# Two alternating places for the first two gate/up chunks, and two experts per loop turn on TensorE and SyncE, in a hybrid decoder step

## The reference

```python
logits = (h @ router_w).astype(jnp.float32) + router_b.astype(jnp.float32)
top_vals, top_idx = lax.top_k(logits, TOP_K)            # 4 of 32 experts per token
gates = jax.nn.softmax(top_vals, axis=-1)
def expert_block(args):
    xb, e = args
    gu = xb @ w_gate_up[e] + b_gate_up[e]               # 1024 x 2048
    g = jnp.minimum(gu[:, :D_FF], SWIGLU_LIMIT)
    u = jnp.clip(gu[:, D_FF:], -SWIGLU_LIMIT, SWIGLU_LIMIT)
    act = (u + 1) * g * jax.nn.sigmoid(SWIGLU_ALPHA * g)
    return act @ w_down[e] + b_down[e]                  # 1024 x 1024
```

## Time and profile before

| | |
|---|---|
| median of the runs | 1736.56 us (1729.86 to 1739.68) |
| the profiled execution's own time | 1735.41 us |
| its span, first to last instruction | 1733.7 us |
| TensorE busy | 1474.0 us (85%), 11950 matmul instructions |
| share of 16 DMA engines, SyncE's queue | 81.9% |
| moved | 598.10 MB, mean 345 GB/s |
| granted TensorE clock, mean | 0.903 of full speed |

### The profile page before, as it was taken

The page is one execution under the profiler, slowest core; times in us unless marked ns, Lnnn a source line. Parts: engine busy times, 40 slices in busy tenths (PEclk is TensorE's granted clock), DMA queues, the critical chain, the costliest instruction groups (busy, mean ns, idle before and its releaser), DMA issues.

```text
span 1733.7 us, 32093 instructions
## 1 busy us (share of the span) xinstructions
PE 1474.0 (85%) x11950; PEld 595.0 (34%) x11951; DVE 782.4 (45%) x1160; ACT 356.0 (21%) x822; POOL 96.7 (6%) x173
## 2 busy tenths in 40 slices
PE   3868887779788978899998998999899999899970
PEld 2433333346433354332332332333233332232320
DVE  2789879997786335221332232132132131131326
ACT  3212212222222111111211211212112122121220
POOL 0000010000000000000100000000000000000000
PEclk8989995679898857999999999999899999999995
DMA  9557888988998785598999999999999999999986
GB/s 327 182 187 258 283 295 272 331 279 292 311 301 270 242 352 207 227 392 339 429 420 403 427 417 396 412 418 411 392 421 412 401 428 411 397 428 399 428 351 253
DMA packets 127292, 598.10 MB, mean 345 GB/s; under 512 B 20503, under 2 KB 20517, under 8 KB 102026
## 3 DMA queue, kind: packets, MB, share of 16 engines
q1 hardware_dynamic: 109088, 560.20, 81.9%
q10 hardware_dynamic: 8634, 20.00, 3.4%
q0 software_dynamic: 9504, 17.06, 2.6%
HBM read 589.36 MB, written 25.87 MB: 355 GB/s over the span
## 4 chain that ended last, share of the span: by engine, by line
PE 40%; DMA 19%; DVE 2%; issue 1%; ACT 0%; DVEq 0%; SPq 0%; ACTq 0%
PE bank L1511 25%; DMA wts<-in_w_gate_up 16%; PE bank L1548 8%; PE bank L1530 4%; DMA wts<-in_w_down 3%; PE bank L1501 1%; PE bank L1618 1%; DVE v_ring L2139 1%; PE bank L1559 1%; PE bank L1599 0%; DVE q_b L2139 0%; DMA h_tok<-h_rows,v_tok 0%; ACT k_T L1155 0%; DVEq L2127 0%; ACT k_T L1138 0%
## 5 line engine op out<-in xcount | busy, mean ns | idle before, releaser
L1511 PE MATMUL bank<-wts,h_T 128*32 128x512 f32 x4032 | 443.9, 597 | 9.7 <-DMA wts<-in_w_gate_up 5.2
L2061 DVE TENSOR_SCALAR q_T<-bank 128x512 f32<-128x512 f32 x32 | 22.1, 692 | 636.9 <-PE bank L1511 636.9
L1511 PEld LDWEIGHTS bank<-wts,h_T 128*32 128x32 f32 x4032 | 129.5, 111 | 308.3 <-issue 296.4
L1548 PE MATMUL bank<-wts,k_T 128*32 128x512 f32 x2048 | 228.3, 597 | 8.0 <-issue 4.9
L1530 PE MATMUL bank<-wts,h_T 128*32 128x512 f32 x992 | 132.6, 675 | 52.2 <-DMA wts<-in_w_gate_up 50.4
L1658 DVE TENSOR_TENSOR wts<-wts,q_b 128x1024 f32<-128x1024 f32 x128 | 158.1, 1235 | 23.1 <-DMA wts<-in_cache_k 17.4
L1661 DVE TENSOR_REDUCE sc<-wts 128x16 f32<-128x1024 f32 x128 | 156.2, 1220 | 4.4
L1145 ACT ACTIVATE h_T<-bank 128x512 f32<-128x512 f32 x66 | 35.9, 595 | 573.5 <-PE bank L1501 573.5
L1548 PEld LDWEIGHTS bank<-wts,k_T 128*32 128x32 f32 x2048 | 64.9, 110 | 149.0 <-issue 139.5
L1223 PE MATMUL bank<-wts,h_T 128*8 128x128 f32 (+1 forms) x480 | 92.7, 465 | 12.3 <-ACT h_T L854 6.4
L1155 ACT ACTIVATE k_T<-bank 32x256 f32<-32x256 f32 x256 | 95.7, 374 | 13.6 <-PE bank L1548 10.2
(11 more groups left out here) (330 smaller groups left out, 1375.8 us busy)
## 6 DMA issues: line engine op xcount, KB each, us to landing
wts<-in_w_gate_up SPq DMA_DIRECT2D x126, 2048.0 KB, 15.8
wts<-in_w_down SPq DMA_DIRECT2D x64, 2048.0 KB, 18.3
wts<-in_cache_k SPq DMA_DIRECT2D x256, 256.0 KB, 3.7
v_ring<-in_cache_v SPq DMA_DIRECT2D x160, 256.0 KB, 3.8
wts<-in_cache_v SPq DMA_DIRECT2D x96, 256.0 KB, 3.9
wts<-in_w_in SPq DMA_DIRECT2D x5, 2048.0 KB, 24.1
wts<-y_rows SPq DMA_DIRECT2D x4, 2048.0 KB, 15.1
wts<-in_w_out ACTq DMA_DIRECT2D x8, 512.0 KB, 6.2
```

Of the source, the lines that this page charges most:

```text
L1511: m = nc.tensor.matmul(PS[part][p0:p0 + 32, :], lhs[:, 32 * b:32 * b + 32], rhs[:, part * F + half * 512:part * F + half * 512 + 512], sta ...
L1548: m = nc.tensor.matmul(PS[4][p0:p0 + 32, :], act_T[0][:, k, a0:a0 + 32], chunk[c][:, k, n * 512:(n + 1) * 512], start=(c == 0 and k == 0), ...
```

## The change

Chunks 0 and 1 of gate/up get a second place each: even places of the order use the old ones, odd places `v_ring` and `mix`, with semaphores of their own (`w_odd`). SyncE may therefore load chunks 0 and 1 of place i as soon as place i-2 has used them. Chunks 2 and 3 and both down chunks have one place, as before; place 1 now has its chunks 0 and 1 loaded early instead of 2 and 3. As the place in memory now depends on the parity of i, the bodies of SyncE's and TensorE's loops are written out for two places of the order per turn. The read of the size moves ahead of the two waits of a block. The last two down chunks wait for place 30 instead of place 31, and the residual rows for place 31's use of chunk 0. Five pairs of semaphores are merged (`rows_in`), to make room.

```diff
+        w_odd = [sem(f"w_odd{n}") for n in range(2)]
+        gu_full = [w_full[0:4], w_odd + w_full[2:4]]
...
-        gu_chunk = [w_slot[CHUNK_SLOT[c]].rearrange("p (k n) -> p k n", k=2) for c in range(4)]
-        first_gu = gu_chunk[0:2] + [v_flat.rearrange("p (k n) -> p k n", k=2),
-                                    mix[:, 0:SLOT].rearrange("p (k n) -> p k n", k=2)]
+        gu_even = [w_slot[CHUNK_SLOT[c]].rearrange("p (k n) -> p k n", k=2) for c in range(4)]
+        gu_odd = [half.rearrange("p (k n) -> p k n", k=2) for half in (v_flat, mix[:, 0:SLOT])] + gu_even[2:4]
+        gu_chunks = [gu_even, gu_odd]
...
-            def load_gate_up(i, e):
+            def load_gate_up(i, e, odd=0, ahead=0):
                 for c in range(4):
-                    sp.wait_ge(w_used[c], i)
-                    load_chunk(c, e)
+                    sp.wait_ge(w_used[c], i - ahead if c < 2 else i)
+                    load_chunk(c, e, odd)
...
             load_chunk(0, 0)
             load_chunk(3, 0)
+            load_chunk(0, 1, 1)
...
-            for c in range(2, 4):
-                sp.wait_ge(w_full[c], 16)
-                load_chunk(c, 1, first_gu)
+            load_chunk(1, 1, 1)
...
+            sp.wait_ge(meta_out, 2)
+            e = expert_at(2)
             for c in range(2):
                 sp.wait_ge(w_used[c], 1)
-                load_chunk(c, 1)
-            sp.wait_ge(meta_out, 2)
-            e = expert_at(2)
+                load_chunk(c, e)
             for c in range(2, 4):
                 sp.wait_ge(w_used[c], 1)
-                sp.wait_ge(w_full[c], 32)
-                load_chunk(c, e)
-            for c in range(2):
+                load_chunk(c, 1, 1)
+            for c in range(2, 4):
                 sp.wait_ge(w_used[c], 2)
                 load_chunk(c, e)
             load_down(1, 1)
-            with sp.Fori(3, E) as i:
-                load_gate_up(i, expert_at(i))
-                load_down(i - 1, expert_at(i - 1))
+            with sp.Fori(3, E - 1, 2) as i:
+                for odd in (1, 0):
+                    load_gate_up(i + 1 - odd, expert_at(i + 1 - odd), odd, 1)
+                    load_down(i - odd, expert_at(i - odd))
             e = expert_at(E - 1)
+            load_gate_up(E - 1, e, 1, 1)
+            load_down(E - 2, expert_at(E - 2))
             for q in range(2):
-                sp.wait_ge(w_used[q], E)
+                sp.wait_ge(w_used[q], E - 1)
...
+            sp.wait_ge(w_used[0], E)
             sp.wait_ge(x2_out, 16 * (TILES + 1))
...
-                    pe.wait_ge(w_full[c], i * 16 + 16)
+                    pe.wait_ge(gu_full[odd][c], loads if c < 2 else i * 16 + 16)
                     for k in range(2):
-                        m = products(hg_T[:, 2 * c + k, :], chunk[c][:, k, :], c == 0 and k == 0, False)
+                        m = products(hg_T[:, 2 * c + k, :], gu_chunks[odd][c][:, k, :], c == 0 and k == 0, False)
...
-            def expert_block(i, before=None, front=gate_up_front, back=gate_up_back):
+            def expert_block(i, before, odd, loads):
...
+                size = size_of(i)
                 after(pe, gclip_done, i * 2)
                 pe.wait_ge(xt_copied, i * 2 + 2)
-                size = by_size(front, back, i)
+                by_size(front, back, i, size)
...
-            expert_block(1, 0, first_gate_up_front, first_gate_up_back)
-            with pe.Fori(2, E) as i:
-                expert_block(i, i - 1)
+            expert_block(1, 0, 1, 16)
+            with pe.Fori(2, E, 2) as i:
+                expert_block(i, i - 1, 0, i * 8 + 16)
+                expert_block(i + 1, i, 1, i * 8 + 16)
```

More of the change, by code:

```diff
@@ L341, in hybrid_step @@
         v_full = [sem(f"v_full{n}") for n in range(VRING)]
-        xw_loaded = [sem(f"xw_loaded{n}") for n in range(TILES + 1)]
+        rows_in = [sem(f"rows_in{n}") for n in range(TILES + 1)]
         win_in = [sem(f"win_in{n}") for n in range(5)]
         w_full = [sem(f"w_full{n}") for n in range(6)]
+        w_odd = [sem(f"w_odd{n}") for n in range(2)]
+        gu_full = [w_full[0:4], w_odd + w_full[2:4]]
         w_used = [sem(f"w_used{n}") for n in range(6)]
-        y_loaded = [sem(f"y_loaded{n}") for n in range(TILES + 1)]
         last_full = [sem(f"last_full{n}") for n in range(2)]
@@ L566, in _, with load_chunk @@
                                                     for part in a_no})
-            def load_chunk(c, e, chunk=gu_chunk):
+            def load_chunk(c, e, odd=0):
                 if c < 4:
@@ L573, in load_chunk @@
                         "a (p k) n -> (a p) k n", p=P)[:, 2 * c:2 * c + 2, :]
-                    sp.dma_start(chunk[c], src).then_inc(w_full[c], 16)
+                    sp.dma_start(gu_chunks[odd][c], src).then_inc(gu_full[odd][c], 16)
                 else:
@@ L1502, in transpose_x, with gate_up_front @@
                     m.then_inc(xt_full, 1)
-            def gate_up_front(i, chunk=gu_chunk):
+            def gate_up_front(i, odd, loads):
                 def products(lhs, rhs, start, stop):
@@ L1522, in gate_up_front, with gate_up_back @@
                 products(sel[0:96, :], b_split[0:96, :], False, True).then_inc(gu_done, 1)
-            def gate_up_back(i, b, chunk=gu_chunk):
+            def gate_up_back(i, b, odd, loads):
                 def products(lhs, rhs, start, stop):
@@ L1534, in gate_up_back @@
                 for c in range(4):
-                    pe.wait_ge(w_full[c], i * 16 + 16)
+                    pe.wait_ge(gu_full[odd][c], loads if c < 2 else i * 16 + 16)
                     for k in range(2):
-                        products(hg_T[:, 2 * c + k, :], chunk[c][:, k, :], c == 0 and k == 0, False)
+                        products(hg_T[:, 2 * c + k, :], gu_chunks[odd][c][:, k, :], c == 0 and k == 0, False)
                 pe.wait_ge(sel_done, i + 1)
@@ L1579, in late_down_back, with size_of, by_size @@
                 down_back(i, b, loads=-1)
-            def by_size(front, back, i, size=None):
-                if size is None:
-                    size = pe.value_load(n_tok[0:1, bass.ds(i, 1)], min_val=0, max_val=CAP)
+            def size_of(i):
+                return pe.value_load(n_tok[0:1, bass.ds(i, 1)], min_val=0, max_val=CAP)
+            def by_size(front, back, i, size):
                 with pe.If(size > 64):
@@ L1589, in by_size @@
                 front(i)
-                return size
             def enter_late():
@@ L1601, in enter_late, with front, back @@
                 m.then_inc(late_summed, 1)
-            def expert_block(i, before=None, front=gate_up_front, back=gate_up_back):
+            def expert_block(i, before, odd, loads):
+                def front(i):
+                    gate_up_front(i, odd, loads)
+                def back(i, b):
+                    gate_up_back(i, b, odd, loads)
+                size = size_of(i)
                 after(pe, gclip_done, i * 2)
                 pe.wait_ge(xt_copied, i * 2 + 2)
-                size = by_size(front, back, i)
+                by_size(front, back, i, size)
                 transpose_x(i + 1)
@@ L1612, in expert_block @@
                 if before is not None:
-                    down_block(before, isinstance(i, int))
+                    down_block(before, isinstance(i, int) and i < 2)
                 for part in range(2):
@@ L1623, in down_block @@
             def down_block(i, first, front=down_front, back=down_back, size=None):
+                if size is None:
+                    size = size_of(i)
                 pe.wait_ge(at_copied, i * 2 + 2)
@@ L1645, in _ @@
                 with pe.If(j < n):
-                    size = expert_block(j + E)
+                    size = expert_block(j + E, None, 0, j * 16 + 16 * (E // 2 + 1))
                     down_block(j + E, False, late_down_front, late_down_back, size)
@@ L1821, in part_w @@
                     if c == 0:
-                        dve.wait_ge(xw_loaded[u], 16)
+                        dve.wait_ge(rows_in[u], 16)
                     if s:
```

12 lines of the change are left out of this document (4 added, 8 removed).

## The result

The changed kernel takes 1916.8 us, the median of 4 runs (1909.2 to 1926.8), against 1735.2 for the kernel before beside it: a ratio of 1.106, 95% interval 1.102 to 1.111. The forecast of 1747 and its range up to 1852 were both too low. The profiled execution's span is 1911.6 us, 177.9 above the 1733.7 of before.

A forecast was written before the change was run, and what follows sets the result against it. Transfers, through the same busy DMA engines, were taken to bound the pairs at 63.8 us. Code refetches of 85.4 us less 75.5 of relief gave +9.9 on 1735.4; 1.2 more for the median made 1747 us, range 1727 to 1852.

The forecast's parts named there:

- The bound of the kernel before: Large/small place pairs, 928 to 1566 us: transfers bound them at 63.8 us, the same engines behind each time.
- of the 31 us little is real: Ten pairs from 928 us: filling the transfer gap could give 31 us at most, but even landings suggest little of it.
- Part 1, gain 5.3 us: Second places for chunks 0 and 1: sooner loads remove place 4's waits and slow clock, 5.3 us gained.
- Part 2, edits at nothing: Moved size read, place 1's chunks, last down chunks, SyncE's longer loop and merged semaphores: 0 us.
- Part 3, twice the code: TensorE's loop body of two places grows from 4 code blocks to 8, 9 wanted; refetching nets +9.9 us.
- If the block at the head of the loop is lost once a turn: TensorE's back edge: one missing block costs 6.1 us at each of 14 back edges, 85.4 us; case's chance 0.40.
- first rival: TensorE's loop loses more than one block per turn, oldest dropped first: +118 us, 1854, middle 1820; chance 0.33.
- the relief of 75.5 us: TensorE's weight waits no longer suffered, 58.7 us, plus slow clock, 12 pairs x 1.4 us, set against the code's cost.
- the 6.18 of the earlier trace: Branch at the loop's entry in the kernel before, transfers busy: 6.18 us, taken as the price of a missing block.
- Straight runs are fetched ahead in time: TensorE's code without jumps: the next block arrives in time, as a block lasts some 13 us.
- about 1 us longer: Back edge of TensorE's loop: a fetch asked for only at the branch takes about 1 us longer; highest price 7.2 us.
- long branches at L1585 in odd places: Sign in TensorE's odd places that would prove that more than one block is lost per turn.

The follow-up runs named there:

- The exchange of the gathers: The parity branch with gathered rows of odd places put on partitions 64 to 127, TensorE's transposes restoring their order: 1713.7 us, ratio 0.990.
- The parity branch: The changed kernel with one place per turn in TensorE's loop, only the products of chunks 0 and 1 standing twice: 1725.8 us, ratio 0.996 to before.
- the kernel with its head at a block's start: The changed kernel with the head of TensorE's loop laid on the first instruction of a code block, nothing else altered: 1866.4 us.
- The hinted kernel without a set head: The changed kernel plus an instruction at the loop's top naming its back edge's target: 1740.5 us in one run, 1736.6 in 12 runs, ratio 1.0018.

## Why the prediction was wrong, point by point

**The bound of the kernel before**: right. The busiest engines set the beat, as the prediction took it from the even landings, and "of the 31 us little is real" held in every kernel whose code stayed. The exchange of the gathers shows it by taking 1.2 us off each pair.

**Part 1, gain 5.3 us**: right in place, and near in size with short code. The parity branch has its first landing 7.3 us earlier and a median 7 us below that of before. In the doubled loop it is about 2.

**Part 2, edits at nothing**: nothing in these runs speaks against it. The parity branch contains all of them and gains.

**Part 3, twice the code**: this is where it failed, in one choice: "If the block at the head of the loop is lost once a turn". The count was right as far as it went (8 blocks of body and a ninth behind its end, as the kernel with its head at a block's start shows with 9 per turn; as laid in the change they are 10), and so was the capacity named as the critical one. The choice of one lost block had no row behind it. A loop that wants more blocks than are held, of which the oldest goes, loses all. The prediction had this as its first rival, at 0.33, priced at 14 x (6.1 + 7.7) - 75.5 = +118.

**The rival's price** was too small by 60 us. What a turn lost was 15.13 + 2.87 = 18.0 us, not 6.1 + 7.7 = 13.8: 14 x 18.0 - 75.5 = +176.5, against 177.9 measured between the spans. So the relief of 75.5 us was right. The branch itself was right too: the back edge lasts 6.2 us at the median, and the 6.18 of the earlier trace rows was the base. By terms, for the turn shown:

| term, us | priced | measured |
|---|---|---|
| idle at the head | 4.4 | 9.29 |
| idle at the odd place's jump | 6.0 | 4.84 |
| idle behind a large place's short jump | 0 | 1.00 |
| lower clock | 2 x 1.7 | 2.87 |

The term that was mis-sized is the head. TensorE waits there for a second fetch in a row, which the sum left out; the kernel whose head lies at a block's start has 4.1 to 5.6 us instead, and by the spans of those two the difference is 47 us. The jump over both backs in the odd place was priced as a landing in a missing block. Its branch lasts only 0.34 us at most in this turn, so it seems to land in a block that is there, with the next one missing: 4.84 us of idleness, eight matmul instructions on. And "Straight runs are fetched ahead in time" holds for most of the code (ten blocks came in this turn, and TensorE stood still at three points), but not behind a large place's short jump over its second back, up to 2.5 us in the sequencer, of which 1.00 us reached TensorE in this turn and 0 to 1.1 in the others. The "about 1 us longer" of a fetch asked for only at the branch was a guess of mine that no row showed: in the change the 14 back edges that waited for a fetch lasted 5.9 to 6.8 us, where the 6.18 of the earlier trace rows was the base.

**The range** ended at that rival's price with one missing block per jump. How code lies in blocks was unknown, so its end should have held two misses in a row.

**The signs named in advance** decided at once, for the first rival: eight or more q8 packets per turn, the back edge at 6 us in every turn, waits for gate/up gone, idleness on "issue". Only "long branches at L1585 in odd places" did not show: the long ones lie at the other branch, in large places.

**What stays open.** The hinted kernel without a set head ran without a fetch, so its body covers 8 blocks at most; the change as made fetches 10 per turn, as a body over 9 would. The two differ by one instruction inside the loop (31965 against 31950 executed, 15 more in 15 turns), and no row shows where a loop's head lies, so why they lie differently isn't settled.

## What to carry to other kernels

Before writing a loop's body out twice, count its instructions against the engine's code memory (8 blocks of 256 instructions on TensorE here), and count the blocks it can cover at its worst position plus one behind its end; over that, the whole body is fetched again in every turn, not the excess (9 or 10 blocks per turn here). A branch around a small part that differs (the parity branch, 1725 us) gives the same freedom for a fraction of the code, and a hint at the loop's top buys one block (8 blocks of body at 1734 us with it, 1866 without). Where a queue of transfers seems to have gaps that nothing fills, look at how small transfers may spread over the DMA engines: moving their rows to other partitions gained 11 us here, a deeper queue 7.

## What the runs showed of the hardware

- TensorE holds 8 blocks of code of 16 KB (0.61 MB in 37 blocks), 256 instructions each (laid from instruction 200 of a block on, TensorE waits for the next one behind 56 more; 5,773 matmul and load instructions came in 23 blocks of straight code, 251 each). In a loop that wants more, none survives. A body over 7 blocks ran with no fetch in the loop, the same code over 8 with 9 per turn, 56 us dearer (one execution each).
- By the counts, the block behind a loop's end is fetched in every turn, and takes a place, unless the back edge is hinted: 8 blocks of body gave 9 fetches per turn without the hint and none with it, and 9 with it gave 9 (1866, 1734 and 1818 us). With the hint, over nine blocks, the head's packet starts 0.02 to 2.3 us before the branch begins and the edge lasts 1.7 us at the median; in the change without it, 3.5 to 4.3 us after, and 6.2.
- A missing block at a back edge costs 6.2 us of the sequencer with the transfers busy. TensorE's own idleness is 4.1 to 5.6 us, or 8.4 to 10.0 where a second fetch follows at once; behind it the granted clock was 0.80 for 8.8 us.
- The partition that a gathered row lands on matters for the transfers beside it. Exchanging the halves for every second place took the pair's beat from 63.7 to 62.5 us, while 5.3 MB of more rows, in small places mostly on partitions 64 to 127, left it within 0.1 us. That it acts through the choice of DMA engines is inferred.
